# First mixer of a fused two-block kernel: inverses of four token chunks stepped together instead of two pairs in turn

## Reference, cut to what matters

```python
def rwkv7_step(S, inp):
    r_t, w_t, k_t, v_t, kk_t, a_t = inp
    sa = jnp.einsum("bhvk,bhk->bhv", S, -kk_t)
    S = (S * w_t[:, :, None, :]
         + jnp.einsum("bhv,bhk->bhvk", sa, kk_t * a_t)
         + jnp.einsum("bhv,bhk->bhvk", v_t, k_t))
    y = jnp.einsum("bhvk,bhk->bhv", S, r_t)
    return S, y
...
def even_mixer(h, w_in, mu, ...):
    proj = h @ w_in
    pa, xb, gb = jnp.split(proj, (A_PROJ, A_PROJ + B_WIDTH), axis=-1)
    ya = rwkv7_time_mix(pa, mu, w0, w2, a0, a2, g2, k_k, k_a, r_k, lnx_g, lnx_b)
    yb = rglru_mix(xb, gb, conv_w, conv_b, gate_a_w, gate_a_b, gate_x_w, gate_x_b, lam)
    return jnp.concatenate([ya, yb], axis=-1) @ w_out
```

## Time and profile before

| | us |
|---|---|
| three runs: median (lowest to highest) | 3565.39 (3559.65 to 3579.29) |
| the profiled execution: first to last instruction (its span) | 3564.1 |
| PE busy, share of the span | 3436.0, 96% |
| DVE busy | 1951.1, 55% |
| ACT busy | 1339.5, 38% |
| mean granted TensorE clock over the span | 0.981 |

### The profile page before, as it was taken

How to read it: one execution, slowest core, us unless ns; L and a number is a source line. 1 busy time by engine, 2 the same in 40 slices (tenths; PEclk the granted TensorE clock), 3 DMA queues, 4 the chain that set the end, 5 groups by cost and what they waited for, 6 DMA issues and landing times.

```text
span 3564.1 us, 48545 instructions
## 1 busy us (share of the span) xinstructions
PE 3436.0 (96%) x20964; PEld 2775.4 (78%) x20964; DVE 1951.1 (55%) x2791; ACT 1339.5 (38%) x2006; POOL 4.0 (0%) x18
## 2 busy tenths in 40 slices
PE   8999996899999999999999999999999999999998
PEld 7888865778888888887578888766888887678887
DVE  6554676456554654253455433566766455866644
ACT  4332464233322433233643322244544233644433
POOL 0000000000000000000000000000000000000000
PEclk9999996899999999999999999999999999999999
DMA  5444330024444342322013232310232231013321
GB/s 189 142 142 147 125 113 20 3 72 145 143 145 142 130 136 95 101 87 81 1 59 101 95 101 103 116 59 25 74 108 97 100 136 66 30 60 101 100 95 60
DMA packets 93094, 342.50 MB, mean 96 GB/s; under 512 B 10320, under 2 KB 10960, under 8 KB 92368
## 3 DMA queue, kind: packets, MB, share of 16 engines
q1 hardware_dynamic: 92880, 339.40, 28.5%
HBM read 337.26 MB, written 2.10 MB: 95 GB/s over the span
## 4 chain that ended last, share of the span: by engine, by line
PE 87%; DVE 7%; ACT 5%; issue 2%; DMA 0%; SPq 0%; DVEq 0%; ACTq 0%
PE ps L774 20%; PE ps L776 20%; PE ps L775 20%; PE ps L810 3%; PE ps L806 3%; PE ps L807 3%; PE ps L845 1%; PE ps L844 1%; PE ps L843 1%; PE ps L1200 1%; DVE SPL L2030 1%; PE ps L1210 1%; ACT WK L1934 1%; PE ps L829 1%; PE ps L830 1%
## 5 line engine op out<-in xcount | busy, mean ns | idle before, releaser
L2030 DVE TENSOR_TENSOR SPL<-RAW,SPH 128x1024 fp32r<-128x1024 f32 x522 | 636.2, 1224 | 1004.2 <-ACT SPH L1444 1004.1
L774 PE MATMUL ps<-HH,SPH 128*128 128x512 f32 x2332 | 919.5, 394 | 9.4 <-DVE SCR L2120 4.6
L1444 ACT ACTIVATE SPH<-RAW 128x1024 fp32r<-128x1024 f32 x522 | 547.8, 1056 | 1008.4 <-PE ps L776 887.9
L776 PE MATMUL ps<-HH,SPL 128*128 128x512 f32 x2332 | 908.5, 390 | 0.0
L775 PE MATMUL ps<-HL,SPH 128*128 128x512 f32 x2332 | 908.3, 390 | 0.0
L774 PEld LDWEIGHTS ps<-HH,SPH 128*128 128x128 f32 x2332 | 438.4, 188 | 112.8 <-issue 10.7
L775 PEld LDWEIGHTS ps<-HL,SPH 128*128 128x128 f32 x2332 | 438.4, 188 | 93.8 <-issue 4.1
L776 PEld LDWEIGHTS ps<-HH,SPL 128*128 128x128 f32 x2332 | 438.2, 188 | 91.9
L774 PE MATMUL ps<-AH,SPH 128*128 128x512 f32 x1008 | 393.6, 391 | 0.0
L776 PE MATMUL ps<-AH,SPL 128*128 128x512 f32 x1008 | 392.3, 389 | 0.0
L775 PE MATMUL ps<-AL,SPH 128*128 128x512 f32 x924 | 359.5, 389 | 0.0
(11 more groups left out here) (491 smaller groups left out, 4203.7 us busy)
## 6 DMA issues: line engine op xcount, KB each, us to landing
RAW<-in_ws SPq DMA_DIRECT2D x522, 512.0 KB, 3.3
RAW<-in_wa SPq DMA_DIRECT2D x96, 512.0 KB, 3.4
WK<-in_sm SPq DMA_DIRECT2D x2, 2784.0 KB, 9.6
WK<-in_cst SPq DMA_DIRECT2D x2, 1664.0 KB, 6.9
X<-in_x SPq DMA_DIRECT2D x8, 256.0 KB, 8.2
out<-X SPq DMA_DIRECT2D x8, 256.0 KB, 2.1
WK<-in_sm SPq DMA_DIRECT2D x1, 768.0 KB, 5.0
PCT<-in_pc SPq DMA_DIRECT2D x1, 349.0 KB, 2.9
```

The lines of the kernel that those rows point to most:

```text
L774: e.matmul(out, wh, rhs[0], start=start, stop=False)
L776: mm = e.matmul(out, wl, rhs[0], start=False, stop=stop)
L1444: e.activation(SPH[:, q:q + 1024], RAW[:, r:r + 1024], ACT.Copy).then_inc(hi_ready.did(("hi", n)))
L2030: e.tensor_tensor(SPL[:, q:q + 1024], RAW[:, r:r + 1024], SPH[:, q:q + 1024].bitcast(F32), ALU.subtract).then_inc(lo_ready.did(("lo", n)))
```

## The change

Pair 1 gets working tiles of its own, in `INV2`, which lies over places 0 to 2 of `SPL`. All engines then run step i for pair 0 and at once for pair 1, with lru as before, and `recurrence_steps()` holds chunks and norms alone. The waits that kept pair 1 behind pair 0 are gone. As `INV2` lies where the low halves of chunks 88 to 90 would be, the four halvings of chunks 88 to 91 (and two blocks of `ADA` before them) move from tiles 18 to 21 to behind steps 1 and 4 of chunks 0 and 1. POOL clears four `T64` instead of two, after the last projection. No product, copy or transfer is added or dropped otherwise. Line numbers of the changed kernel are one or two higher.

```diff
             if c < 2:
-                yield "inverse", 1, STEPS_CHUNK * c + i
             yield "chunk", c, i
...
-        SPL, _ = place("SPL", NSPL * CH * 128, F32R)
+        SPL, spl_at = place("SPL", NSPL * CH * 128, F32R)
+        INV2, _ = place("INV2", 6 * T, at=spl_at)
...
+        inv = {"W": [SCR[:, c * T:(c + 1) * T] for c in range(2)] + [INV2[:, c * T:(c + 1) * T] for c in range(2)],
+               "WP": [SCR[:, 0:2 * T], INV2[:, 0:2 * T]], "LD": [ACC[:], INV2[:, 4 * T:5 * T]],
...
                 for i in range(STEPS_INV):
-                    inverse(0, i)
+                    for p in range(2):
+                        inverse(p, i)
                     for j, part in LRU_AT.get(i, ()):
                         lru(j, part)
...
                 for i in range(22):
-                    halve_to(ahead_of(s, i))
+                    halve_to(min(ahead_of(s, i), BASE[s] + 21))
...
-                    if what == "inverse":
-                        inverse(c, i)
-                    elif what == "chunk":
+                    if what == "chunk":
                         chunk(c, i)
+                        if c < 2 and i in (1, 4):
+                            halve_to(BASE[s] + 22 + 2 * c + i // 4)
...
-                            w.wait_ge(("nm", c, lv),
-                                      *([("dd", c, lv - 1)] if lv > 1 else [("dd", c - 2, 5)] if p else []))
+                            w.wait_ge(("nm", c, lv), *([("dd", c, lv - 1)] if lv > 1 else []))
...
-                w.wait_ge(("bon", 3))
-                for c in range(2):
+                w.wait_ge(("bon", 3), ("proj", s, 21))
+                for c in range(4):
                     m = e.memset(u8(inv["T64"][c], slice(0, 32), 32), 0.0)
```

More of the change, by code:

```diff
@@ L371, in build @@
                 rwkv["MX"][name, hf] = wk(30 + 3 * hf + i)
-        inv = {"W": [SCR[:, c * T:(c + 1) * T] for c in range(2)], "LD": ACC[:],
-               "NM": [WK[:, 38 * T + 800 + 256 * c:38 * T + 1056 + 256 * c] for c in range(2)],
-               "T64": [SCR[:, (2 + c) * T:(3 + c) * T] for c in range(2)],
+        inv = {"W": [SCR[:, c * T:(c + 1) * T] for c in range(2)] + [INV2[:, c * T:(c + 1) * T] for c in range(2)],
+               "WP": [SCR[:, 0:2 * T], INV2[:, 0:2 * T]], "LD": [ACC[:], INV2[:, 4 * T:5 * T]],
+               "NM": [WK[:, 38 * T + 800 + 256 * c:38 * T + 1056 + 256 * c] for c in range(2)] +
+                     [INV2[:, 5 * T + 256 * c:5 * T + 256 * c + 256] for c in range(2)],
+               "T64": [SCR[:, (2 + c) * T:(3 + c) * T] for c in range(2)] +
+                      [INV2[:, (2 + c) * T:(3 + c) * T] for c in range(2)],
                "TT": [(YLa if c < 2 else YLb)[:, c % 2 * 2 * T:(c % 2 + 1) * 2 * T] for c in range(4)]}
@@ L1657, in inverse @@
                             w.wait_ge(("nm", c, 5), ("dd", c, 4))
-                            e.activation(inv["NM"][c % 2], ps["nm", c, 5][:, 0:256], ACT.Copy).then_inc(
+                            e.activation(inv["NM"][c], ps["nm", c, 5][:, 0:256], ACT.Copy).then_inc(
                                 act_done.did(("nmc", c, 5)))
@@ L1662, in inverse @@
                             b, TTc = ps["dd", c, 5], inv["TT"][c]
-                            w.wait_ge(("dd", c, 5), *([("nm", c - 2, 6)] if p else []))
-                            e.activation(u8(inv["T64"][c % 2], slice(32, 64)), u8(b[:, 0:256], slice(32, 64)), ACT.Copy)
+                            w.wait_ge(("dd", c, 5))
+                            e.activation(u8(inv["T64"][c], slice(32, 64)), u8(b[:, 0:256], slice(32, 64)), ACT.Copy)
                             e.activation(u8(TTc, slice(64, 96), 96), u8(b[:, 0:256], slice(64, 96)), ACT.Copy)
@@ L1669, in inverse @@
                         for c in pair:
-                            w.wait_ge(("nm", c, 6), *([("dd", c - 2, 6)] if p else []))
-                            e.activation(inv["T64"][c % 2][64:128, :], ps["nm", c, 6][64:128, :], ACT.Copy).then_inc(
+                            w.wait_ge(("nm", c, 6))
+                            e.activation(inv["T64"][c][64:128, :], ps["nm", c, 6][64:128, :], ACT.Copy).then_inc(
                                 act_done.did(("nmc", c, 6)))
```

29 lines of the change are left out of this document (14 added, 15 removed).

## The result

| | us |
|---|---|
| before: median (lowest to highest, runs) | 3564.77 (3557.95 to 3579.29, 20) |
| the change: median (lowest to highest, runs) | 3576.66 (3571.77 to 3581.08, 20) |
| ratio after to before, 95% interval | 1.0031 [1.0025, 1.0037] |
| forecast | 3568.5 (3552 to 3582) |

A forecast was written before the change was run, and what follows sets the result against it. The prediction took PE's instruction stream to bound the levels. Its terms, 23.5 + 90.5 + 20.8 + 30.5 + 2.5 = 167.8 against 160.2, less 4.5 of head, gave +3.1 us: 3568.5, range 3552 to 3582.

The forecast's parts named there:

- the pace: Added instruction packets: by the slowest window they cost 2.0 us more, by the fastest 2.1 less.
- the bank: Lru's first products: a wait for a bank that ACT frees late, bounded by 0 and 2.4 us, taken as 0.
- the clock in chunk 0: Upper end of the range: half of the low clock's cost, in chunk 0, +4 us.
- What bounds the levels: Levels: PE's instruction stream, 128 records in 3.74 us; pair 1 adds 44.9 us to 45.6, giving 90.5.
- the first rival: Levels: issue waits are unnamed handovers between engines, which a second pair covers, 28.2 us, giving 3540; chance 0.09.
- Head: Before the inverse: halvings leave DVE's tiles 18 to 21, so the inverse starts 4.5 us earlier.
- The third rival: Before the inverse: something else holds the first product back, +4.5 us gives 3573; chance 0.10.
- First products and lru: Start of the inverse: with pair 1's records added, 15.2 us becomes 23.5.
- Joining: End of the inverse: pair 1's busy time less a covered wait of 2.3 us, 13.1 + 7.7 = 20.8.
- Chunk 0: After the inverse: it runs alone with no norm beside it, 13.2 us.
- the second rival: Chunks 0 and 1: PE stays at 1.2 GHz through both, 17.8 us more, 3586; chance 0.07.
- Moved halvings and chunk 1: Chunk 1: an ADA block and a low half before the norm's first step on DVE, +2.5 us.

The follow-up runs named there:

- the well placed halvings: Kernel before with only the four late halvings moved, ahead of steps 0 and 6 of chunk 0: 3559.21 us (ratio 0.9989), again 3558.18 (0.9984).
- the first experiment: Kernel before with only the four late halvings moved, to the places the change gives them: 3565.23 us against 3564.58, ratio 1.0004.

## Why the prediction was right, and where its sum fell short

The sum gave a change of 3.1 us, and the medians moved by 11.9. The sign and what bounds the stage are those of the forecast. That the time lies inside the range is owed to the width of its upper end, 13.5 us for the pace, the halvings, the bank and the clock in chunk 0, and not to the sum; for the joining, which came out longest against its term, the range had only less time, not more.

**What bounds the levels: right.** The forecast took "issue" for PE's instruction stream, against the first rival (waits between engines, 3540). With a second pair the waits for DVE went and issue grew; the pace stayed at 3.7 to 3.8 us a packet; the waits came once a packet; doubling products at four packets cost 14.5 us against the 15 that the pace gives, and 14 us of PE's work on top cost 2.6. The levels came out at 90.7 and 89.5 for 90.5. The rule of the Trainium skill ("Runtime: NRT & Kernel Launch", section Instruction fetch mechanics) that the next block is fetched while the current one runs, and that this is mostly hidden, does not hold for these products as to the hiding: by it the doubled ones would have run in the waits, nearly free.

**Head: right.** The gap fell from 5.56 to 0.86 us, 4.7 for 4.5, with no wait ahead of the first product. The third rival (the head start does not come) falls with it. That it can be kept, and is worth 6 us alone, the well placed halvings show.

**First products and lru: 1.9 and 0.3 short.** The wait for the bank, which I took as 0 between 0 and 2.4, was 0.7 (line 964 in the waits after). The rest goes with the clock, 0.73 in one profile and 0.86 in the other. The first 32 records of the inverse before, and pair 1's 32 after:

```profile
539.10 3.79 PE L978 MATMUL ps<-WK 64*128 64x128 f32 x32 [4.70 <-DVE WK L2234]
...
543.41 3.78 PE L979 MATMUL ps<-WK 64*128 64x128 f32 x32
```

Before, they took 3.79, not the 3.38 that I read at another place, so 0.4 more was saved there than I took off; pair 1's took 3.78 where I gave them 2.06.

**Joining: 2.9 and 2.2 short, the step that failed.** "Pair 1 adds that busy time, less the 2.3 that pair 0 waited for line 2326, now covered by the other chunks: 13.1 + 7.7 = 20.8." It took 23.7 and 23.0. That wait was covered, but 2.9 us of issue at lines 1018, 1046 and 1022 took its place: I let the second pair fill a wait for DVE here, which in the levels I had refused to do for this very reason. PE's busy time, 20.9 for twice 10.03, goes with the clock: 0.50, where pair 0's stretch had 0.58. So 2.1 of the 2.9 are waits and 0.8 is busy time.

**Chunk 0: 2.7 and 1.6 short.** I gave it 13.2 from chunk 2's rows at full clock. Its first products came out of the joining at the lower level, in PE's order of time:

```profile
676.29 5.48 PE L979 MATMUL ps<-WK 64*128 64x128 f32 x48
```

48 at the full clock are 3.1 (2.06 x 48 / 32), so 2.4 of the 2.7 are here. It is the second rival (the clock stays low into the chunks) in small: some 6 us of it, not two chunks. I had put 4 for this into the range, not into the sum, though the earlier trace rows showed 3.38 for 2.06 at that very place.

**Moved halvings and chunk 1: the wait right, what follows it missed.** An ADA block and a low half stand before the norm's first step on DVE as I said, and PE's wait grew from 0.81 to 3.13, 2.3 for 2.5. PE in order of time behind it:

```profile
699.57 2.08 PE L1134 MATMUL ps<-SCR,CST 128*128 128x512 f32 x2 [3.13 <-ACT SCR L1697]
701.44 1.91 PE L1064 MATMUL ps<-CST,WK 128*128 128x128 f32 x8
703.14 1.92 PE L1139 MATMUL ps<-WK 128*128 128x128 f32 x8
```

Lines 1134 and 1139 have 1.13 and 1.06 in the earlier trace rows: these products ran at the lower level, and with line 1064 (1.04 in chunk 2) gave away some 2.7 us more. In the second profile the wait was the same and less was lost behind it, 1.4 in the three lines:

```profile
694.75 1.12 PE L1134 MATMUL ps<-SCR,CST 128*128 128x512 f32 x2 [3.13 <-ACT SCR L1697]
...
697.08 1.92 PE L1139 MATMUL ps<-WK 128*128 128x128 f32 x8
```

The wait was priced, its effect on the clock was not; the same pair, a wait and slow products behind it, ate the head start in the first experiment.

Together the joining, chunk 0 and chunk 1 are 8.3 of the 10.5 us by which the first profile exceeds the sum (178.3 against 167.8); in the second they are 5.2 over, of which the levels gave 1.0 back (172.2). So the inverse ended at 676.3 and 672.7 for the 670 I named, and chunk 2 began 15.4 and 9.3 us after 699.3, where I had said within 10. In both the sign and the mechanism are those of the forecast, a stream-bound stretch made longer by lost mixing; the sizes that failed are the joining's waits for issue and those that depend on the clock behind the levels.

## What to carry to other kernels

Where PE waits for "issue" in many small products and the instruction queue ticks at a constant pace, more independent small products cannot fill the waits; put large products there instead, and count records, not busy time. Price a new wait of PE with the products behind it at the lower clock, which here added 1.4 to 3 us to a wait of 2 to 3. When a transfer or a copy is moved to a place "beside other work", look for the in-order engine that waits for its partner there: a halving is an ACT copy, a DVE subtraction and a load, and each of the three held up somebody in one of these runs.

## What was not expected of the hardware

A wait of PE of 2 to 3 us was followed by products at the lower clock level: 2.04 us cost some 3 more in the first experiment, 3.13 us 2.7 more in chunk 1 of the change and 1.4 in its second profile; with 0.8 in its place the stretch of chunk 1 had a clock of 1.00. Wide products nobody reads raised the granted clock of the levels from 0.58 to 0.75 without making them shorter, and the joining behind them was as slow as before (23.6 us at 0.50). And one kernel's stage from the first product to chunk 2 took 178.3 and 172.2 us in two profiles, two thirds of the difference lying where the clock rows differ.
